# Decay sums of a state-space scan: loaded cumulative sums with a maximum, in place of a triangular matmul; the masked product on GpSimd

## The reference, cut to what matters

```python
acum = jnp.cumsum(dt * A.reshape(g, r), axis=2)
seg = acum[:, :, :, None] - acum[:, :, None, :]
decay_ls = jnp.exp(jnp.where(causal[None, None, :, :, None, None], seg, -jnp.inf))
cb = jnp.einsum('bclgn,bcsgn->bclsg', C, B)
y_diag = jnp.einsum('bclsgr,bcsgrp->bclgrp', cb[..., None] * decay_ls, xdt)
```

## Time and profile before

| what | value |
|---|---|
| three runs | 2917.32, 2922.39, 2913.11 us (median 2917.32) |
| profiled execution | 2906.55 us |
| its span, first to last instruction | 2904.7 us |
| mean granted TensorE clock | 0.94 of full speed |
| TensorE matmul busy | 2541.9 us (88%) |
| VectorE busy | 1412.6 us (49%) |
| ScalarE busy | 1032.9 us (36%) |
| GpSimd busy | 394.2 us (14%) |

### The profile page before, as it was taken

How to read it: one execution, slowest core, us unless ns; L and a number is a source line. 1 busy time by engine, 2 the same in 40 slices (tenths; PEclk the granted TensorE clock), 3 DMA queues, 4 the chain that set the end, 5 groups by cost and what they waited for, 6 DMA issues and landing times. The chain is left out here.

```text
span 2904.7 us, 39007 instructions
## 1 busy us (share of the span) xinstructions
PE 2541.9 (88%) x12894; PEld 2066.1 (71%) x12894; DVE 1412.6 (49%) x3081; ACT 1032.9 (36%) x2154; POOL 394.2 (14%) x287
## 2 busy tenths in 40 slices
PE   4799799799799859999999999979988787758598
PEld 4777687687596548877788888868978765446366
DVE  3456365455455523333645777406666531176411
ACT  3244235235235322332423333316667742210400
POOL 0024014004104200000211433110000000011000
PEclk9899899899899979999999999989999988879699
DMA  3110310220221283320123322222333553242201
GB/s 102 55 40 26 97 44 22 77 71 19 61 76 33 60 266 82 89 88 29 58 106 120 109 74 105 78 77 64 80 84 96 126 150 103 67 171 74 95 0 61
DMA packets 213688, 235.10 MB, mean 81 GB/s; under 512 B 29463, under 2 KB 155279, under 8 KB 212520
## 3 DMA queue, kind: packets, MB, share of 16 engines
q1 hardware_dynamic: 213544, 233.21, 26.3%
HBM read 172.27 MB, written 64.69 MB: 82 GB/s over the span
## 5 line engine op out<-in xcount | busy, mean ns | idle before, releaser
L697 PE MATMUL bank<-wh,uH 128*128 128x512 f32 x792 | 308.4, 389 | 0.0
L699 PE MATMUL bank<-wh,uL 128*128 128x512 f32 x792 | 308.1, 389 | 0.0
L698 PE MATMUL bank<-wl,uH 128*128 128x512 f32 x792 | 308.1, 389 | 0.0
L2110 PE MATMUL bank<-uH,wxh 128*128 128x364 f32 (+1 forms) x576 | 193.5, 336 | 15.2 <-issue 10.3
L1251 ACT ACTIVATE sc<-sc,nmx 128x128 f32<-128x128 f32 (+1 forms) x384 | 169.7, 443 | 103.6 <-DVE nmx L1324 102.5
L2112 PE MATMUL bank<-uH,wxl 128*128 128x364 f32 (+1 forms) x576 | 192.2, 334 | 4.9 <-issue 4.9
L2111 PE MATMUL bank<-uL,wxh 128*128 128x364 f32 (+1 forms) x576 | 192.8, 335 | 0.0
L699 PEld LDWEIGHTS bank<-wh,uL 128*128 128x128 f32 x792 | 148.7, 188 | 30.9
L698 PEld LDWEIGHTS bank<-wl,uH 128*128 128x128 f32 x792 | 148.7, 188 | 30.8
L697 PEld LDWEIGHTS bank<-wh,uH 128*128 128x128 f32 x792 | 148.7, 188 | 30.7
L1420 PE MATMUL bank<-kT,qT 128*128 128x128 f32 (+1 forms) x768 | 165.7, 340 | 1.3 <-ACT qT L1220 1.3
(11 more groups left out here) (307 smaller groups left out, 5533.4 us busy)
## 6 DMA issues: line engine op xcount, KB each, us to landing
yin<-scratch_yT SPq DMA_DIRECT2D x16, 1024.0 KB, 5.8
wr<-in_a_in_w SPq DMA_DIRECT2D x8, 2048.0 KB, 9.5
wx<-in_m_in_w SPq DMA_DIRECT2D x26, 512.0 KB, 3.8
scratch_q<-rot SPq DMA_DIRECT2D x48, 256.0 KB, 2.0
qn<-scratch_q SPq DMA_DIRECT2D x48, 256.0 KB, 3.5
scratch_u<-ub SPq DMA_DIRECT2D x48, 256.0 KB, 2.9
u<-scratch_u SPq DMA_DIRECT2D x24, 512.0 KB, 4.8
h<-in_x_prompt SPq DMA_DIRECT2D x2, 4096.0 KB, 19.7
```

The lines of the kernel that those rows point to most:

```text
L697: pe.matmul(bank[:, t % 3, :], high, whigh, start=(k == 0), stop=False)
L698: pe.matmul(bank[:, t % 3, :], high, wlow, start=False, stop=False)
L699: last = pe.matmul(bank[:, t % 3, :], low, whigh, start=False, stop=(k == KT - 1))
L2110: pe.matmul(to, wxh[:, f % 2, k, :], uH[:, k, c0:c1], start=(k == 0), stop=False)
```

## The change

The decay sums are no longer made by TensorE. Ahead of the loop the cumulative sums are also made transposed (a head per partition, negated by ScalarE into `acT`), stored to memory (`scratch_acum`) and, in the other layout, kept negated in `nac`. For every chunk SP loads the row of cumulative sums of the 8 heads, broadcast to all partitions, straight into `mix` (`load_decay`). VectorE takes the maximum with the partition's own sum (`bound_decay`, one chunk ahead; the maximum keeps the exponent from being positive where the mask is zero), and ScalarE's exponential subtracts through its bias, head by head: eight instructions of 128 columns in place of one of 1024. The masked product goes from VectorE to the head of GpSimd's part of the chunk; GpSimd's `decay_sums` and TensorE's L2163 and L2165 go. ScalarE waits for `sum_ready` (VectorE) in place of `seg_full` (TensorE).

```diff
@@ -227,6 +227,8 @@
         ea = sb("ea", [P, NT, NH])
+        nac = sb("nac", [P, NT, NH])
+        nacg = sb("nacg", [P, NT, HG])
@@ -256,6 +258,7 @@
         sdec = sb("sdec", [P, XF, NSEQ])
+        acT = xbc[0:NH, 0:2, :].rearrange("p a b -> p (a b)")[:, 0:NT * P]
@@ -284,12 +287,13 @@
             wz_landed wo_landed nw_landed xg_full raw_ready conv_done conv_ready
         q = {n: sem(n) for n in names.split()}
+        decay_landed = [sem(f"decay_landed{i}") for i in range(2)]
@@ -1692,7 +1696,24 @@
             sp.wait_ge(u_ready, NT)
+            sp.wait_ge(q["turned_ready"], 5)
+            for g in range(NG):
+                sp.dma_start(s["acum"][g].rearrange("t h l -> h t l"),
+                             acT[g * HG:(g + 1) * HG, :].rearrange("h (t l) -> h t l", t=NT)).then_inc(q["cw_loaded"], 16)
+            sp.wait_ge(q["cw_loaded"], 48 + 16 * NG)
+            def load_decay(g, c):
+                r = ROWS[c]
+                src = s["acum"][bass.ds(g, 1), c, :, 0:r]
+                sp.dma_start(mix[0:r, c % 2, 0:HG * r].rearrange("p (h l) -> p h l", h=HG),
+                             src.broadcast_to([r, HG, r])).then_inc(decay_landed[c % 2], 16)
             with sp.Fori(0, NG) as g:
+                sp.wait_ge(q["yd_full"], g * NT)
+                alone(sp)
+                load_decay(g, 0)
+                load_decay(g, 1)
@@ -1726,6 +1747,10 @@
                 for c in range(LC):
+                    if c + 2 < NT:
+                        sp.wait_ge(q["yd_full"], g * NT + c + 1)
+                        alone(sp)
+                        load_decay(g, c + 2)
@@ -1768,22 +1793,16 @@
-            def decay_sums(g, c, n):
-                r = ROWS[c]
-                alone(pool)
-                tri = con("tri" if c < LC else "tri8", r)[:, 0:r]
-                out = mix[0:r, c % 2, 0:HG * r].rearrange("p (h l) -> p h l", h=HG)
-                pool.tensor_tensor(out, over(tri, r, HG, r), bc(dta[0:r, c, bass.ds(g * HG, HG)], r, HG, r),
-                                   ALU.mult).then_inc(q["sum_ready"], 1)
                     r = ROWS[c]
-                    if c == 0:
-                        pool.wait_ge(q["yd_full"], n)
-                        decay_sums(g, 0, n)
+                    pool.wait_ge(q["e_ready"], n + 1)
+                    pool.wait_ge(q["cbm_ready"], n + 1)
+                    if c == LC:
+                        alone(pool)
+                    mv = mix[0:r, c % 2, 0:HG * r].rearrange("p (h l) -> p h l", h=HG)
+                    pool.tensor_tensor(mv, mv, over(cbm[0:r, 0:r], r, HG, r), ALU.mult).then_inc(q["m_ready"], 1)
@@ -1797,10 +1816,6 @@
                                        bc(dend[0:r, c, bass.ds(g * HG, HG)], r, HG, HD), ALU.mult).then_inc(q["xdtd_ready"], 1)
-                    if c + 1 < NT:
-                        if c:
-                            pool.wait_ge(q["yd_full"], n)
-                        decay_sums(g, c + 1, n + 1)
@@ -1833,6 +1848,11 @@
             act.activation(vec[:, NH:2 * NH], vec[:, NH:2 * NH], ACT.Exp).then_inc(q["acum_ready"], 1)
+            act.wait_ge(q["acum_full"], 3)
+            for x in range(3):
+                w = min(4 * P, NT * P - 4 * P * x)
+                last = act.activation(acT[:, 4 * P * x:4 * P * x + w], bank[0:NH, 1 + x, 0:w], ACT.Copy, scale=-1.0)
+            last.then_inc(q["turned_ready"], 1)
@@ -1855,7 +1875,9 @@
                 act.copy(cwg[:, XF, :], cwv[:, bass.ds(g + NG * XF, 1), :].rearrange("p f k -> p (f k)"))
-                act.copy(cwg[:, XF + 1, :], cwv[:, bass.ds(g + NG * XF + NG, 1), :].rearrange("p f k -> p (f k)")).then_inc(q["cwg_ready"], 1)
+                act.copy(cwg[:, XF + 1, :], cwv[:, bass.ds(g + NG * XF + NG, 1), :].rearrange("p f k -> p (f k)"))
+                act.copy(nacg[:, :, :], nac[:, :, bass.ds(g * HG, HG)]).then_inc(q["cwg_ready"], 1)
+                act.wait_ge(q["cwg_ready"], g + 1)
@@ -1899,11 +1921,11 @@
                     act.copy(btok[0:r, :], bank[0:r, 1, 0:DS]).then_inc(q["btok_ready"], 1)
-                    act.wait_ge(q["seg_full"], n + 1)
-                    if c < LC:
-                        act.activation(mix[:, c % 2, :], bank[:, 2:4, :].rearrange("p b n -> p (b n)"), ACT.Exp).then_inc(q["e_ready"], 1)
-                    else:
-                        act.activation(mix[0:r, c % 2, 0:HG * r], bank[0:r, 2, :], ACT.Exp).then_inc(q["e_ready"], 1)
+                    act.wait_ge(q["sum_ready"], n + 1)
+                    for hh in range(HG):
+                        v = mix[0:r, c % 2, hh * r:(hh + 1) * r]
+                        last = act.activation(v, v, ACT.Exp, scale=-1.0, bias=nacg[0:r, c, hh:hh + 1])
+                    last.then_inc(q["e_ready"], 1)
@@ -1944,6 +1966,7 @@
             chain(dve.memset(tiny[:, :, :], 0.0))
+            chain(dve.memset(nac[:, :, :], 0.0))
@@ -1965,6 +1988,7 @@
             for r, c0, c1 in ((P, 0, PT * NH), (SAMP, PT * NH, n)):
+                dve.tensor_scalar(nac[0:r, :, :].rearrange("p t h -> p (t h)")[:, c0:c1], bank[0:r, 5, c0:c1], -1.0, None, ALU.mult)
@@ -1975,7 +1999,16 @@
+            def bound_decay(g, c):
+                r = ROWS[c]
+                dve.wait_ge(decay_landed[c % 2], 16 * (5 - c % 2) * g + 16 * (c // 2 + 1))
+                alone(dve)
+                v = mix[0:r, c % 2, 0:HG * r].rearrange("p (h l) -> p h l", h=HG)
+                dve.tensor_tensor(v, v, bc(nacg[0:r, c, :], r, HG, r), ALU.max).then_inc(q["sum_ready"], 1)
             low_x(0, 0)
+            dve.wait_ge(q["cw_loaded"], 48 + 16 * NG)
@@ -2007,6 +2040,7 @@
                 low_x(g + 1, 0)
+                bound_decay(g, 0)
@@ -2019,10 +2053,8 @@
                     dve.tensor_tensor(hv(xdt[0:r, :]), hv(xt[0:r, :]), bc(dtv[0:r, c, hs], r, HG, HD), ALU.mult).then_inc(q["xdt_ready"], 1)
-                    dve.wait_ge(q["e_ready"], m + 1)
-                    dve.wait_ge(q["cbm_ready"], m + 1)
-                    mv = mix[0:r, c % 2, 0:HG * r].rearrange("p (h l) -> p h l", h=HG)
-                    dve.tensor_tensor(mv, mv, over(cbm[0:r, 0:r], r, HG, r), ALU.mult).then_inc(q["m_ready"], 1)
+                    if c + 1 < NT:
+                        bound_decay(g, c + 1)
@@ -2095,7 +2127,13 @@
                 last.then_inc(q["acum_full"], 1)
+            for t in range(NT):
+                r = ROWS[t]
+                m = con("tri") if t < PT else con("tri8", r)[:, 0:r]
+                last = pe.matmul(bank[0:NH, 1 + t // 4, t % 4 * P:t % 4 * P + r], dta[0:r, t, :], m, start=True, stop=True)
+            last.then_inc(q["acum_full"], 1)
             pe.wait_ge(q["acum_ready"], 5)
+            pe.wait_ge(q["turned_ready"], 5)
@@ -2155,15 +2193,6 @@
                     pe.matmul(bank[0:r, 1, DS:DS + r], xbc[:, XF, cs], xbc[:, XF + 1, cs], start=True, stop=True).then_inc(q["bc_full"], 1)
-                    pe.wait_ge(q["sum_ready"], n + 1)
-                    if c == LC:
-                        alone(pe)
-                    if c < LC:
-                        for half in range(2):
-                            last = pe.matmul(bank[:, 2 + half, :], con("after"), mix[:, c % 2, 512 * half:512 * (half + 1)], start=True, stop=True)
-                    else:
-                        last = pe.matmul(bank[0:r, 2, :], con("after8", r)[:, 0:r], mix[0:r, c % 2, 0:HG * r], start=True, stop=True)
-                    last.then_inc(q["seg_full"], 1)
@@ -2252,7 +2281,7 @@
 _SCRATCH = {"yT": (DI, TOK), "kv": (TOK, 2, NGR, KVH * HD), "q": (TOK, NGR, D), "gate": (TOK, D), "u": (NGR, SEQ, D), "ms": (NGR, SEQ, 2 * AH),
-            "os": (SAMP, D)}
+            "os": (SAMP, D), "acum": (NG, NT, HG, P)}
```

More of the change, by code:

```diff
@@ L286, in trunk_kernel @@
             wz_landed wo_landed nw_landed xg_full raw_ready conv_done conv_ready
-            x_full xt_ready bc_full btok_ready cbm_ready sum_ready seg_full e_ready m_ready z_full z_ready
+            x_full xt_ready bc_full btok_ready cbm_ready sum_ready e_ready m_ready z_full z_ready
             xdt_ready xdtd_ready skip_ready yd_full st_full hT_ready gated ssy_ready msy_ready ry_ready yn_ready
```

## The result

The changed kernel takes 3000.38 us (median of 4 runs, 2999.01 to 3005.45) where the kernel before, on the same chip, took 2916.62 (4 runs): ratio 1.0288, 95% interval 1.0267 to 1.0309. It is 83.8 us slower; 40.8 was forecast, and 3000 lies above the range of 2930 to 2985. The profiled execution took 3005.45 (span 3003.7 against 2904.7); the two spans differ by 99.0, of which 15 is where the two profiled executions lie among their runs: the one of before is 10 us under its median, this one 5 over.

A forecast was written before the change was run, and what follows sets the result against it. TensorE bounds a chunk at 12.04 us; after the change a loop over the engines does, at 13.1. Terms 22.1 + 11.3 + 11.6 - 5.2 - 5.0 + 6.0 = +40.8 on 2917.3 give 2958 us, range 2930 to 2985.

The forecast's parts named there:

- the exponentials: ScalarE, each chunk: eight of 128x128 in place of one of 128x1024 take 2.50 us instead of 1.03, +1.47.
- the load: Broadcast row of sums for each chunk: 512 KB lands in 3.8 us, costing only from about 11.9 us on.
- the setup: Before the loop, once: 18 matmul passes, three copies to acT, a negation and a memset, +6.0 us.
- (3): First chunk of each group: slower exponentials and product, wait for the maximum, possible low clock; 2.9 x 4 = +11.6 us.
- (5): End of a group: L2057 no longer runs beside GpSimd's product; -1.7 in three groups, -5.0 us.
- Term (1): Seven steady intervals in each of four groups: the loop needs 13.07, say 13.1 us a chunk; +22.1 us.
- the mask at 1.89: Masked product moved to GpSimd, each chunk: 1.89 us, taken from the removed product, against 1.23 on VectorE, +0.66.
- rival B: GpSimd's mask is slower, as with two full operands: 0.52 more in 32 chunks, +17, 2975 us; chance 0.12.
- Term (2): Steady chunks: TensorE's 2.8 us gap lowers the clock in half of 28, +0.8 us each in L2219; +11.3 us.
- Term (4): Last chunk of each group (sample rows): VectorE's preparation 1.3 us earlier, GpSimd's mask done first; -1.3 x 4 = -5.2 us.
- TensorE's need of 10.32: Steady chunk: TensorE's own work falls from 12.04 to 10.32 us, far less than the loop needs.
- the 1.72 us taken off: TensorE, each chunk: removing the two fp32 matmuls L2163 saves 1.32 + 0.40 = 1.72 us.

The follow-up runs named there:

- the last experiment: Twelve unread TensorE products in each ninth chunk, added to the kernel with early exponentials (first chunk's during the projection) and masked product on VectorE: 2872.16 us, ratio 0.9837.

## Why the prediction was wrong: right in kind, wrong in its terms

**Right.** The loop became the bound, the removed matmuls saved nothing, TensorE waits for GpSimd in every chunk, the load is hidden, the maximum delays nobody in the steady chunk. Three terms held: the exponentials (2.50 forecast, 2.45), the load (3.8, 3.7) and the setup (+6.0 forecast; +5.4 at the first projection product, +5.7 at the end of the first projection). So did the mechanism at the end of a group, where the collision of 2.43 is gone:
```profile
600.27 0.74 DVE L2089 SCALAR_TENSOR_TENSOR square<-square,ybuf,gain 64x512 f32<-64x512 f32 x1 [0.65 <-POOL ybuf L1820]
```

**Terms (3) and (5), first chunk and end of a group: each 7 us off, and the sum right by luck.** Forecast were 11.6 and -5.0; the traces have 18.7 and -11.5. The first chunk of the second group:
```profile
439.11 1.23 DVE L2000 TENSOR_TENSOR wxl<-wx,wxh 128x1024 fp32r<-128x1024 f32 x1 [2.11 <-ACT wxh L1904]
...
446.43 2.07 PE L2244 MATMUL bank<-gain,xbc 128*128 128x512 f32 x2 [7.24 <-POOL mix L1805]
```
From the end of L2000 (440.34) to L2244 it is 6.09 us, where it was 3.28 before (416.74 to 420.02): 2.8 a group, near the 2.5 forecast. But behind the pause of 7.24 both matmul groups start at the low clock in all four first chunks (granted 0.50), and from L2244 to the power it is 9.84 us where it was 7.3 to 8.3: 7.5 in the four groups, where 1.6 was forecast. On the other side, the stretch from the ninth power to the last L2000 of the next group's projection became 3.4 to 4.3 us shorter and not 1.7: a pause of 1.5 to 1.7 in the first block of the projection (L2112) is gone too. Why it is gone wasn't tried.

**Term (1), the interval: 22.1 forecast, 37.8 measured** (28 x 13.65 = 382.2, less 344.4). The step that failed is the mask at 1.89, taken from "the same tile and sizes". The removed product's operand repeats along a row and the mask changes with every column, which made that row a bad neighbour: (2.35 - 1.89) x 28 is 12.9 us. That was rival B, which was given 0.12, and the remark that the repeated operand "runs differently" was the warning. The page "GPSIMD Engine Reference" of the Trainium skill (3.1, Elementwise), whose ratio of 1.96 gave 2.41, was nearer than the row for this form; for the other form the trace has 1.90, so the ratio doesn't hold for every product. Of the 0.12 us of the interval over 13.07 + 0.46, 0.09 is the stretch from L2244 to L2076, 2.97 at the full clock behind a pause where it was 2.88 without one; it is there with the shorter product too (13.18 against 13.07).

**Term (2), the clock: 11.3 forecast, 26.6 measured** (408.8 - 382.2). Half of the chunks was right, by luck: the reason, the turns that the pauses take, the prediction didn't have. The size failed: 0.8 was the difference of L2219 alone, between a row at 2.70 and one at 1.89. But 2.70 lies between the levels, a row in which the clock changed on the way (mean granted 0.66 over it); wholly at the low one L2248 takes 3.51 for 1.89, and L2244 ahead of it 2.07 for 1.12. The loop loses up to 5.50 - 2.97 = 2.53 us, and 1.9 on average over the 14. Both are some 1.85 times the full-clock duration: with two levels a factor of two apart, the low price could have been bounded by doubling the full-clock rows, for both matmul groups.

**Term (4), the ninth chunk: -5.2 forecast, +16.4 measured,** the wrong sign. The first half came about: the product that took 2.06 takes 1.21.
```profile
561.20 1.21 DVE L2061 TENSOR_TENSOR u<-btok,cst 64x1024 f32<-64x1024 f32 x1
...
562.69 1.28 POOL L1805 TENSOR_TENSOR mix<-mix,cbm 64x512 f32<-64x512 f32 x1 [2.93 <-ACT mix L1927]
...
562.98 3.23 DVE L2064 COPY u<-xbc 128x8 f32<-128x8 f32 x8
...
563.93 1.03 POOL L1809 TENSOR_TENSOR xt<-xt,vec 64x512 f32<-64x512 f32 x1
...
564.93 1.03 POOL L1816 TENSOR_TENSOR xdtd<-xdt,dend 64x512 f32<-64x512 f32 x1
...
566.68 1.03 PE L2209 MATMUL bank<-cst,u 64*128 64x8 f32 x8 [2.55 <-DVE u L2065]
...
568.53 2.08 PE L2231 MATMUL bank<-u,xdtd 64*128 64x128 f32 x8
...
571.59 1.97 PE L2237 MATMUL bank<-h0T,u 128*64 128x512 f32 x2
```
```profile
564.30:574.00 9.70, 7.32 (x28) 4.84 (x29) 3.81 (x10) 1.85 (x4) 1.66 (x2) 0.68 0.16 50
```
But the prediction let GpSimd's mask be "done first" and didn't ask what then stands behind it. The exponentials of 64 columns take 2.02 us in eight parts, so the mask begins only at 562.69, and the mask, skip and xdtd products now lie beside VectorE's eight small copies: 3.23 us for them, where they take 0.87 in the last experiment, with only the tail of a GpSimd product beside them. They end 0.25 us after GpSimd's last product (566.21, 565.96). That one causes the other is read from this order; it was not tried by itself. So the first sample product (L2209) starts 7.46 us behind the eighth power, where it started 6.55 behind it before: VectorE's part is 0.9 later and not 1.3 earlier. TensorE's pause grew from 2.06 to 2.55, and the first sample products behind it ran at half speed, which adds 2.1 up to the ninth power; together they are the +3.0 of this group (40.47 against 37.48). Over the four groups the later start is 3.6 of the 16.4. The other 12.8 lie behind it, at a mean granted clock of 0.75 to 0.83 against 0.91 to 1.00 before; the prediction had put the clock in this chunk at nothing. The last experiment shows the clock as the cause with the mask on VectorE. That a filled pause gives it back with the mask on GpSimd was not tried.

Together: 15.7 from the interval, 15.3 from the clock, 21.6 from the ninth chunk, 0.4 net from the first chunks, the ends of the groups and the setup, 5.2 from behind the last power: 58.2, the distance from 40.8 to 99.0. TensorE's need of 10.32 was not put to the test, as the loop sets the pace in every changed kernel here. The rows agree with the 1.72 us taken off: from the product of B and C to the second product of z it was 2.18 before (L2157 at 463.59, L2125 at 465.77) and is 0.46 now (L2195 at 466.77, L2163 at 467.23).

## What to carry to other kernels

When an engine gets work off the path and a loop over several engines becomes the bound, ask what its new pause does to it: here the longer loop cost 37.8 us by itself and another 26.6 by the clock that fell behind 14 of 16 pauses of 1.9 to 3.05 us, while behind the 12 pauses of up to 1.52 us it stayed up. An engine that the profile shows as busy for 79.38 of 80 us may still be waiting: the start of its instruction against the end of what it waits for tells it. Work that needs only early data (the exponentials) belongs ahead of a wait on the loop and not behind it; moved there, and with the masked product back on VectorE, the same change went from 2.9% slower to 0.7% faster, and to 1.2% with the first chunk's taken forward too. For a price from a neighbouring row, the way each operand runs counts as much as its shape, and a row at a changing clock is no price for the low one.

## What was unexpected of the hardware

- More work on TensorE made the kernel faster, twice: 12 unread products ahead of the wait of each chunk took 17 to 20 us off the changed kernel (by the medians, or against the kernel before of each), and 12 in each ninth chunk took 14.9 off another version (2887.02 to 2872.16).
- A chunk at the low clock mostly protects the next one, since its late end shortens the next pause (15 of 16); 14 of 28 intervals were long.
- GpSimd's product of 128x1024 takes 1.90 us with an operand that repeats along a row, 2.35 with one that changes with each column, and 2.68 (mean) where it starts just behind VectorE's xdt. VectorE's maximum, 1.22 alone, takes 3.39 when it starts behind that product.
